# Router logits by token, the last expert pair by quarters, and a new order of the first steps: a two-layer kernel on one core

## The reference

```python
y = xf * lax.rsqrt(jnp.mean(xf * xf, axis=-1, keepdims=True) + NORM_EPS)
return (y * g.astype(jnp.float32)).astype(x.dtype)              # rmsnorm
...
g_logits = (hf @ w_rg + b_rg)                                   # 4 groups
g_sel = jnp.argmax(g_logits, axis=-1)
p_group = softmax(g_logits)[g_sel]
e_logits = (jnp.einsum('td,gde->tge', hf, w_re) + b_re)         # 4 x 8 experts
top_vals, top_idx = lax.top_k(e_logits[g_sel], 2)
weight = p_group * jax.nn.softmax(top_vals, axis=-1)
...
return (jax.nn.silu(xb @ w_g[e]) * (xb @ w_u[e])) @ w_d[e]      # one expert, width 256
...
out = x + moe(rmsnorm(x, ffn_norm)); result = rmsnorm(out, final_norm)
```

## Time and profile before

| | before |
|---|---|
| median of 3 runs | 746.95 us |
| profiled execution | 748.94 us |
| its span | 747.1 us |
| PE, DVE, ACT, POOL busy | 89%, 52%, 45%, 53% |
| mean granted TensorE clock | 0.978 |
| moved by DMA | 181.68 MB |

### The profile page before, as it was taken

The page is one execution under the profiler, slowest core; times in us unless marked ns, Lnnn a source line. Parts: engine busy times, 40 slices in busy tenths (PEclk is TensorE's granted clock), DMA queues, the critical chain, the costliest instruction groups (busy, mean ns, idle before and its releaser), DMA issues.

```text
span 747.1 us, 13776 instructions
## 1 busy us (share of the span) xinstructions
PE 666.2 (89%) x5578; PEld 554.3 (74%) x5578; DVE 388.1 (52%) x664; ACT 333.6 (45%) x611; POOL 392.8 (53%) x284
## 2 busy tenths in 40 slices
PE   2999989989999999989999999998899997777754
PEld 2999879879989999988879998995654543343321
DVE  5899963599995247976855554624311110010002
ACT  7456657855653457554358665342212111111102
POOL 3789647687879989797798556970000000000000
PEclk9899999999999999999999999999999999999997
DMA  9735323433434554543454333799799999999992
GB/s 323 289 125 206 123 89 139 150 132 121 162 121 169 188 201 169 170 144 139 148 191 169 114 114 131 308 421 421 264 423 418 421 421 421 422 420 422 421 415 81
DMA packets 26129, 181.68 MB, mean 243 GB/s; under 512 B 2896, under 2 KB 3152, under 8 KB 4688
## 3 DMA queue, kind: packets, MB, share of 16 engines
q1 hardware_dynamic: 26064, 180.77, 63.2%
HBM read 179.71 MB, written 1.05 MB: 242 GB/s over the span
## 4 chain that ended last, share of the span: by engine, by line
PE 56%; DVE 19%; DMA 12%; issue 4%; ACT 4%; POOL 2%; SPq 2%; ACTq 0%; DVEq 0%
PE D L449 30%; PE L L880 5%; DVE big L1401 4%; DMA xT<-w_expert_dram 4%; DMA hT<-w_expert_dram 4%; DMA big<-w_expert_dram 4%; PE L L860 3%; PE QB L910 3%; DVE small L1401 2%; POOL ring_r L1384 2%; PE D L489 2%; PE D L917 2%; PE L L606 1%; SPq L388 1%; DVE big_r L1420 1%
## 5 line engine op out<-in xcount | busy, mean ns | idle before, releaser
L1384 POOL TENSOR_TENSOR ring_r<-ring,ring_r 128x512 fp32r<-128x512 f32 x280 | 392.6, 1437 | 108.6 <-ACT ring_r L1000 108.5
L449 PE MATMUL D<-scr_r,ring_r 128*128 128x256 f32 x1104 | 213.1, 289 | 0.7 <-DVE big L1401 0.7
L1000 ACT ACTIVATE ring_r<-ring 128x1024 fp32r<-128x1024 f32 x140 | 146.2, 1053 | 79.8 <-PE D L449 70.2
L449 PEld LDWEIGHTS D<-scr_r,ring_r 128*128 128x128 f32 x1104 | 175.3, 191 | 3.4 <-issue 2.1
L449 PE MATMUL D<-hT_r,ring_r 128*128 128x256 f32 x552 | 156.1, 283 | 0.0
L449 PE MATMUL D<-big_r,ring_r 128*128 128x256 f32 x1110 | 140.2, 287 | 4.4 <-POOL ring_r L1384 4.3
L449 PEld LDWEIGHTS D<-big_r,ring_r 128*128 128x128 f32 x1110 | 136.7, 195 | 6.7 <-POOL ring_r L1384 3.9
L449 PEld LDWEIGHTS D<-hT_r,ring_r 128*128 128x128 f32 x552 | 105.7, 192 | 1.2 <-issue 1.0
L1401 DVE SCALAR_TENSOR_TENSOR th<-th,L 64x256 f32<-64x256 f32 x32 | 13.4, 418 | 179.4 <-ACT th L1315 178.9
L1315 ACT ACTIVATE th<-L 64x256 f32<-64x256 f32 x16 | 6.0, 378 | 85.1 <-PE L L880 85.1
L860 PEld LDWEIGHTS L<-cst,big 128*128 128x128 f32 x256 | 29.8, 191 | 12.3 <-issue 12.3
(11 more groups left out here) (339 smaller groups left out, 1005.7 us busy)
## 6 DMA issues: line engine op xcount, KB each, us to landing
ring<-w_dense_dram SPq DMA_DIRECT2D x69, 1024.0 KB, 5.0
big<-w_expert_dram SPq DMA_DIRECT2D x40, 1024.0 KB, 24.9
ring<-w_expert_dram SPq DMA_DIRECT2D x30, 1024.0 KB, 26.5
wu<-w_expert_dram SPq DMA_DIRECT2D x6, 1024.0 KB, 24.6
attn<-w_expert_dram SPq DMA_DIRECT2D x5, 1024.0 KB, 20.2
scr<-w_expert_dram SPq DMA_DIRECT2D x5, 1024.0 KB, 27.0
hT<-w_expert_dram SPq DMA_DIRECT2D x5, 1024.0 KB, 27.3
xT<-w_expert_dram SPq DMA_DIRECT2D x5, 1024.0 KB, 27.6
```

The lines of the kernel that those rows point to most:

```text
L449: last = mm(out_, r32(w[i][ws]), r32(x[j][xs_]), start=start and m == 0, stop=stop and m == 2)
L1000: A_(r32(hi_unit(j)), dense_unit(j), ACT.Copy).then_inc(hi_ready, 1)
L1384: last = g.tensor_tensor(r32(w), w, r32(h).bitcast(F32), ALU.subtract)
```

## The change

It has four parts.

1. **Start.** The two transfers of x go to ScalarE's queue. ScalarE rounds unit 1 ahead of x's squares. VectorE's small steps stand ahead of x's chunks.
2. **Router by token.** The router's weights are multiplied by the norm's gain once, on VectorE, in layer two's middle. Logits are formed from the un-normed xT with xT as the stationary operand (`route`), two chunks at a time, so that tokens are on the partitions from the start; three of the four calls can stand between or right behind the dense chunks. The squares are summed by token as well (`sum_tokens`), the 1/rms is one number per partition, and VectorE applies it with the bias in two instructions. `htok` is read from the four banks that already hold x by token, scaled by 1/rms; its gain is applied by `stage`, which moves from ScalarE to VectorE. The transposes of hT and of the logits are gone. The second gather goes to the bank QB rather than wait for L0.
3. **Expert panels.** Panels 0, 1 and 2 go to `wu`, `scr` and `hT` and are issued from unit 124 on; 17 is issued with the last dense units and only 18 waits for x to be in PSUM.
4. **Tail by quarters.** Down weights are packed by half of the columns instead of by expert. The last pair's down, copy and addition are done for each half of the columns (`last_down`, `last_combine`), with the addition of pair 14 ahead of the last gate and up half. The squares of the first half of the columns run while the second half is added. The root's table is loaded behind the last tanh, one root and one reciprocal serve both token halves, VectorE makes two output quarters and ScalarE the other two, which go out on ScalarE's queue.

```diff
@@ SyncE
             for h in range(2):
-                sp_.dma_start(xT[:, 4 * h:4 * h + 4, :], x_t[...]).then_inc(s_in[f"x{h}"], 16)
                 sp_.dma_start(dense_unit(h), w_dense[0][:, h * UNIT:(h + 1) * UNIT])...
...
+            dense(left.pop(0))
+            dense(left.pop(0))
+            sp_.wait_ge(unit_done, UNIT0["omoba"])
             expert(0)
             expert(1)
             dense(left.pop(0))
             expert(2)
+            dense(left.pop(0))
+            sp_.wait_ge(o_mm, H1 + 2 * H2)
             expert(3)
+            expert(4)
...
-            sp_.wait_ge(ssq, N_FFN + 1)
-            expert(16)
-            sp_.wait_ge(htok_mm, 4)
-            expert(17)
-            sp_.wait_ge(x2_in, 1)
+            sp_.wait_ge(x2_in, 4)
             expert(18)
@@ TensorE
+            def route(i):
+                kept(pe, "out2", i)
+                for c in (2 * i, 2 * i + 1):
+                    for tt in range(NT):
+                        mm(OB[:, tt * 64:tt * 64 + NG + NE], xT[:, c, tt * P:(tt + 1) * P], wrt[:, c, :],
+                           start=(c + tt == 0), stop=(c == DC - 1), skip_group_check=True)
+            def sum_tokens(c0):
+                for c in (c0, c0 + 1):
+                    for tt in range(NT):
+                        last = mm(OB[:, P + tt:P + tt + 1], x1_sq[:, c, tt * P:(tt + 1) * P], ones[:, 0:1], ...)
             for c in range(2, 8):
                 chunk("out2", c, (m2_hi, tg2))
-            sumsq(N_FFN)
...
+                if c in (3, 5, 7):
+                    route(c // 2 - 1)
+            pe.wait_ge(folded, 3)
+            sum_tokens(0)
+            route(3)
+            pe.wait_ge(sq, SQ0[N_FFN] + 4)
+            sum_tokens(6).then_inc(ssq, 1)
@@
-            gather(0, 1)
-            sw_transposes(0)
             pe.wait_ge(flagged, 1)
+            gather(0, 1)
             uncrowded = pe.value_load(rt[0:1, 544:545].bitcast(I32), min_val=0, max_val=1)
@@
                 gate_up_half(p, 0, x).then_inc(panel_used, 2)
+                pe.wait_ge(xe_ready, 2 * (p // 2) + 2)
+                if p + 1 == PAIRS:
+                    combine(p - 1)
                 gate_up_half(p, 1, x).then_inc(gu_done, 1)
@@
+            def last_combine(h):
+                pe.wait_ge(ye_ready, PAIRS + h)
+                for turn in range(2):
+                    if turn:
+                        pe.wait_ge(half_added, 2 * h + 2)
+                    for tt in range(NT):
+                        q = (tt + turn) % 2
+                        rows = slice(2 * WIN * q, 2 * WIN * (q + 1))
+                        mm(ACC[tt][h][:, q * 256:(q + 1) * 256], swT[rows, ...], ye[rows, ..., h * 256:(h + 1) * 256],
+                           ...).then_inc(x2_ready if turn else half_added, 1)
@@ ScalarE
+            for h in range(2):
+                act.dma_start(xT[:, 4 * h:4 * h + 4, :], x_t[...]).then_inc(s_in[f"x{h}"], 16)
...
+            advance(2)
             squares(N_X, x_in)
-            advance(2)
@@
-            squares(N_FFN, x1_src(act, "out2"))
-            rootmean(N_FFN)
+            A_(stat[:, 0, 2, 0:1], sp[:, 9, 0:1], ACT.Sqrt)
+            squares(N_FFN, x1_src(act, "out2"), x1_sq)
+            act.wait_ge(ssq, N_FFN + 1)
+            A_(rt[:, 850:852], OB[:, P:P + 2], ACT.Sqrt, bias=sp[:, 9, 0:1], scale=1.0 / D).then_inc(rooted, 1)
+            act.wait_ge(rinvd, N_FFN + 1)
             for n in range(4):
-                act.wait_ge(htok_mm, n + 1)
-                A_(htok[...], LB[n % 2][:, :], ACT.Copy).then_inc(htok_ready, 1)
+                h, tt = n // 2, n % 2
+                act.wait_ge(x2_in, n + 1)
+                A_(htok[:, tt, h * 512:(h + 1) * 512], ACC[tt][h][:, :], ACT.Copy,
+                   scale=rt[:, 848 + tt:849 + tt]).then_inc(htok_ready, 1)
@@ VectorE
+            v.tensor_tensor(wrt[:], wrt[:], V("ffn_norm_2", 0, 8).unsqueeze(2).to_broadcast([P, DC, NG + NE]),
+                            ALU.mult).then_inc(padz, 1)
...
+            v.reciprocal(rt[:, 848:850], rt[:, 850:852]).then_inc(rinvd, 1)
+            for tt in range(NT):
+                last = stt(lgs[:, tt, 0:NE + NG], OB[:, tt * 64:tt * 64 + NE + NG], rt[:, 848 + tt:849 + tt],
+                           V("b_router", 0, NE + NG), ALU.mult, ALU.add)
...
+            def stage(g, half):
+                dve.wait_ge(gathered, 2 * g + half + 1)
+                ...
+                v.tensor_tensor(xe[:, g % 2, 4 * half:4 * half + 4, :], (QB if 2 * g + half == 1 else X)[:, :]...,
+                                V("ffn_norm_2", 4 * half, 4)..., ALU.mult).then_inc(xe_ready, 1)
```

More of the change, by code:

```diff
@@ L855, in gather @@
                 pe.wait_ge(picked, g + 1)
-                if 2 * g + half:
+                if 2 * g + half > 1:
                     pe.wait_ge(xe_ready, 2 * g + half)
+                into = DN if 2 * g + half == 1 else X
                 for c in range(4):
                     for tt in range(NT):
-                        last = mm(X[:, c * P:(c + 1) * P], htok[:, tt, (4 * half + c) * P:(4 * half + c + 1) * P],
+                        last = mm(into[:, c * P:(c + 1) * P], htok[:, tt, (4 * half + c) * P:(4 * half + c + 1) * P],
                                   sel[:, g % 2, tt, :], start=(tt == 0), stop=(tt == NT - 1))
@@ L945, in _ @@
                         pe.wait_ge(ye_ready, p)
[L946 removed]
                     if p + 1 < PAIRS:
+                        down(p, p % 2).then_inc(y_mm, 1)
                         sw_transposes(p + 1, release=2)
[L949 to L952 removed]
+                last_down(0)
+                last_down(1)
+                last_combine(0)
+                last_combine(1)
             with pe.Else():
@@ L1030, in x_in @@
                 return xT[:, c:c + w, :]
+            for h in range(2):
+                act.dma_start(xT[:, 4 * h:4 * h + 4, :], x_t[:, 4 * h * T:4 * (h + 1) * T].rearrange(
+                    "p (c t) -> p c t", c=4)).then_inc(s_in[f"x{h}"], 16)
             act.wait_ge(sp_step, 2)
```

279 lines of the change are left out of this document (142 added, 137 removed).

## The result

The changed kernel takes 738.06 us (median of 4 runs, 735.73 to 739.29) against 746.92 for the kernel before on the same chip: ratio 0.9873, 95% interval 0.9849 to 0.9897. It is faster by 8.9 us, and I had forecast 15.7. The time lies above my range of 727.5 to 736.

The account below looks back on a forecast made before the run. The expert stage's panel transfers, a stream of fixed length between the chain to the first slot release and a tail, bound the kernel. Start 3.8, router 9.0 and tail 2.9 made 15.7 us: 746.95 to 731.3, range 727.5 to 736.

Parts of the forecast that it names:

- Start: From x's landing through the first units: rounding order and clock together win 3.8 us, bounds 0 and 5.5.
- Unit 1's rounding ahead of the squares: At the start: ScalarE rounds unit 1 before squaring x, so TensorE starts it 2.0 to 2.1 us earlier.
- The clock: At unit 1's 24 matmuls: a shorter TensorE gap may keep 2.4 GHz, winning 1.8 us, bounds 0 and 2.6.
- VectorE's small steps: At the start: about 10 steps of 0.2 us moved into VectorE's wait for x, worth 0 before and after.
- x on ScalarE's queue: At the start: no change of x's landing taken; bounds 1.2 us later and 1.5 earlier.
- the start gives nothing: Rival: x lands a microsecond later, the clock drops all the same; start 0.5, time 734.6 us, chance 0.17.
- Router: From the dense matmuls' end to the first slot release: 18.1 us instead of 27.1, 9.0 earlier, bounds 7.5 and 10.
- The branch: In the router: TensorE's flag load now stands directly ahead of gate and up, costing 0.3 us, bounds 0 and 1.
- Panels earlier: Before the expert stage: early panels are absorbed, the first 19 in by about 523 us instead of 531.
- Stream: Expert stage: after the first release, 77 panels at 421 GB/s take a fixed 191.9 us.
- Tail: From the last gate and up half to the end: 2.9 us won, bounds 1.5 and 3.5.
- Sum: Whole kernel: 3.8 + 9.0 + 2.9 = 15.7 us won, median from 746.95 to 731.3.

Follow-up runs that it names:

- e1: The kernel before with only the change's start (x on ScalarE's queue, unit 1 rounded first, VectorE's small steps early): 746.88 us, ratio 0.9995.
- e10: The changed kernel with all three parts of the start put back as before: 736.27 us, ratio 0.9841.
- e8: The kernel before, unchanged, executed and profiled a second time: 744.96 us, one run.
- e6: The changed kernel with unit 1 rounded behind x's squares again: 736.74 us, ratio 0.9863.
- e9: The changed kernel with the second pair of slots given back earlier, by the first transpose of the slot weights: 735.73 us, ratio 0.9836.
- e5: The changed kernel with x back on SyncE's queue behind vec: 737.31 us, ratio 0.9862.
- e0: The changed kernel run again without any edit: 737.40 us, ratio 0.9854.
- e11: The changed kernel with the old slot order and the old places of the first panels' issues: 737.73 us, ratio 0.9860.
- e12: The changed kernel with token sums over 128 columns, the earlier second slot release and all outputs issued by SyncE: 735.04 us, ratio 0.9845.
- e13: As e12, plus four unread matmuls in the last pair's wait, against the changed kernel: 734.38 us, ratio 0.9838.
- e2: The changed kernel with the token sums' matmuls over 128 columns of ones instead of 1: 737.35 us, ratio 0.9847.

## Why the prediction was wrong, step by step

**Start: forecast 3.8, measured 0.1 (e1), and e10 agrees.** This is the step that failed, in both its halves.
- "Unit 1's rounding ahead of the squares: TensorE starts 2.0 to 2.1 earlier." With the change's order it started at 17.2 to 18.25 in eleven profiles, with the old order at 18.17, 17.53 (e8), 18.20 (e10) and 17.99 (e6); 16.2 was forecast. VectorE's last product for x ended between 15.5 and 15.9 in all eleven; the rest of the scatter is the pace of unit 0's last eight matmuls:

```profile
16.41 1.71 PE D L521 x8
```

```profile
16.19 0.99 PE D L521 x8
```

The first is the changed kernel, the second e9; why the pace differs was not found (the granted clock stands at 1.00 there in the first). I followed the chain of the earlier trace rows through GpSimd and did not ask who else was nearly as late. GpSimd's work, moved up, fell on VectorE's products, which took 1.4 us each instead of 0.8 (four in 5.57; in the kernel before four in 3.08). The Trainium skill, "SBUF — State Buffer", section "SBUF: two separate sides", says that GpSimd and VectorE, when VectorE reads two operands from SBUF or runs in a mode that uses both of its ports, share one pair of ports, and that the one which comes second waits for the other's whole instruction. The traces agree: steps of 8 columns take 0.17 us with GpSimd idle and 1.1 to 1.2 beside it, about one GpSimd instruction (1.25). In the kernel before:

```profile
18.60 0.17 DVE L1453 TENSOR_TENSOR sp<-sp 128x8 f32<-128x8 f32 x1
18.62 5.00 POOL L1384 TENSOR_TENSOR ring_r<-ring,ring_r 128x512 fp32r<-128x512 f32 x4 [0.50 <-ACT ring_r L1000]
18.80 1.14 DVE L1454 TENSOR_TENSOR sp<-sp 128x8 f32<-128x8 f32 x1
```

- "The clock: 1.8." Here I counted one piece of luck twice. The profiled execution of before had 5.49 for the 24 matmuls, and it lay 2.0 above the median. I booked 1.8 as something the change wins, and then took 2.0 off for the median. The second execution, with 3.13, took 744.96. The 24 matmuls vary from one execution to the next in either kernel (before: 5.49 and 3.13; with the change or parts of it: 3.2 to 4.6).
- "VectorE's small steps: worth 0 both before and after." True only under the slow clock, which covered them. With the clock up, before, they cost 1.05 (e8).
- "x on ScalarE's queue: I take no change of its landing." x's second half came at 9.06 (8.6 to 9.2 in the profiles with two queues) instead of 10.35; in one queue it came at 9.69 in e8, 10.37 in e10 and 9.54 in e5. So it landed 0.5 to 1.3 earlier, inside my bounds, and the estimate "up to 1 us later and not earlier" did not come out. It was worth nothing, because ScalarE rounded unit 0 until 9.78 and VectorE came after. The second queue also delayed vec from 2.8 to 5.0, without effect on unit 1.

The rival "the start gives nothing" had 0.17 and 734.6. It was right about the start and for another reason than the one I gave it: x did not land later, VectorE was in the way. The time is still 2 to 3.5 us above it, by the terms below.

**Router: forecast 9.0, measured 7.9 in the first profile and in e0, 9.5 to 10.25 in the others.** Counted from where the dense matmuls would have ended without two calls of `route` among them (507.54 less 1.62 is 505.92), MAX8 came at 6.66, forecast 6.7, and the onehot at 9.87, forecast 9.9. Counting came at 12.0 instead of 9.9, because L842's transposes took 6.4 us at 0.50 instead of the 3.7 I had from the earlier trace rows. Release at 19.2, forecast 18.1. In the five profiles without the drop it is 16.9, because the steps behind the counting took 7.2 instead of the 8.2 I had added up. In the kernel before, twice, and in e1 with its router, the distance was 27.14, 27.13 and 27.11. The chain was right, with TensorE's clock as the term I had left out. The branch cost nothing that shows: gate and up begin as the second gather ends, forecast 0.3.

**Panels earlier: absorbed**, as forecast; the slots were full at 523, and the transfers stood for 3 to 4 us. e11 shows them to be worth 1.5 to 2.

**Stream: forecast unchanged, measured 0.9 longer.** From release to last half it was 191.6 and is 192.5; since this distance was 192.1 in e8 and 193.0 in e1, with the old slots, I go by the bytes of the first ten microseconds. The forecast had left out what the change does to the second release: with the slot weights' transposes behind the first gate and up it came 3.97 behind the first instead of 3.78, and 0.86 us of transfers are missing; releasing it earlier brings them back (e9, e12, e13).

**Tail: forecast 2.9.** The clean distance is from the release to the end, since the bytes between are the same: before 211.85 and 211.93, in e1 with the old tail 211.55; with the new slots and tail 209.9 to 210.6 at full clock in the last down, and 212.0 to 212.25 at the low one (the first profile, e2 and e5). With the pit taken out, the tail gives 1.8 to 2.9 at full clock and about 0.5 at the low one. The steps, in e6 at full clock: the squares began 3.4 behind the start of down (3.2), ScalarE's last issue came 8.6 behind it (8.15), and its scaling took 0.72 each (0.6). I had 0.1 to 0.2 for outputs that leave together, at most 1; before, the span ended 3.3 behind the last product, now 4.5 to 5.25 behind ScalarE's last issue. So from the start of down to the end I had 11.6 us, and it is 13.1 to 13.7 at full clock, against 14.0 before (13.7 in e1). That the whole still has the forecast size is luck. Down began 197.9 behind the release before and 196.7 to 197.0 now, and 195.6 to 195.8 in the three runs without the pit: 2.1 to 2.3 earlier, where I had 0.5. I had carried over 3.31 us for the last gate and up half, whose clock had fallen in that execution, as a stretch of it shows; it takes 1.97 now.

```profile
728.00:729.00 1.00, 1.00 (x15) 0.57 (x11) 0.00 (x0) 0.00 (x0) 0.00 (x0) 0.50 0.59 246
```

In the kernel before a full clock there would not have helped: in e1 this half began later behind the release, ran at the faster pace, and down then waited 0.62 for its panel and began 197.9 behind the release all the same.

**Sum.** 0 + 10.2 + 2.5 - 0.9 = 11.8 in an execution without drops of the clock, 735.2 from 747; a drop takes 0.7 to 2.4 back. One of them gives 736 to 737.6, and the changed kernel's three medians are 738.06, 737.40 and 736.86. Two executions fit drop by drop: the first profile had the router's 2.4 and the last down's 1.7 to 2.1, which makes 739.3 to 739.7, measured 739.29; e0's had the router's alone, 737.6, measured 737.10.

## What to carry to other kernels

Look into a second execution before you book a stall as something to win: what only one of them shows is luck, and a forecast that starts from the median must not win it again. Before you move an engine's work ahead, list the steps that end within a microsecond or two of it, and those that share a port with it. Where a queue restarts from empty, look at the second release as well as at the first: moving it 2.0 us forward brought back 0.9 us of transfers here.

## What the runs showed of the hardware

- The granted clock fell to 0.50 while TensorE was busy in every one of the microseconds before, with matmuls of 1 and 36 float32 columns (509 to 511 in the changed kernel). With the sums over 128 columns it stood at 1.00 in the stretches shown and the router's length was the same in three profiles. Why it falls in some executions and not in others is open.
- A distance in the program can be exact to 0.1 us from execution to execution (27.14, 27.13, 27.11) while the whole moves by 4 us, because executions differ in a few places only: at the start, at one wait near 100 us, in the router and in the tail. Distances in a trace settled what medians with a spread of 2 to 7 us could not.
- With the second pair of reissues 3.97 us behind the first, 315 to 323 GB/s were moved in the ten microseconds from the first; 2.0 us earlier it was 355 to 359. What happens in the queues when they run dry was not measured by itself.
- VectorE's steps of 8 columns took 0.17 us with GpSimd idle and 1.1 to 1.2 beside it; four of its products of 256 columns took 1.67 with GpSimd idle (from 7.30 on in the kernel before) and 5.57 beside it (in the changed kernel).
